# The layer norms' gain and bias as columns of the turned rows, the residual rows finished on GpSimd

## The chip, the core and the metric

The kernel runs on one core of a Trainium2 chip. The metric is the device time of one execution in microseconds (us). Engines are named as the profile names them: PE is the TensorE matmul, PEld its weight load, DVE is VectorE, ACT is ScalarE, POOL is GpSimd, SP is SyncE, whose queue issues the large weight loads.

## The reference

The program is a first block of four sublayers (hybrid attention, dense, state space, experts; only the extra row block below touches them) and then a second block of two equal layers. One layer of the second block is:

```
def layer_norm(x, g, b):
    xf = x.astype(jnp.float32)
    mu = xf.mean(-1, keepdims=True)
    var = jnp.square(xf - mu).mean(-1, keepdims=True)
    return ((xf - mu) * lax.rsqrt(var + LN_EPS) * g + b).astype(x.dtype)

def hybrid_layer(x, w_in, ..., w_out, ln1_g, ln1_b, w_up, ffn_conv_w, ffn_conv_b, w_down, ln2_g, ln2_b, pos):
    proj = x @ w_in
    ...
    mix = jnp.concatenate([o_a, o_b], -1) @ w_out
    x = layer_norm(DEEPNORM_ALPHA * x + mix, ln1_g, ln1_b)
    hid = causal_dwconv(x @ w_up, ffn_conv_w) + ffn_conv_b
    gate, val = jnp.split(hid, 2, -1)
    ffn = (jax.nn.silu(gate) * val) @ w_down
    return layer_norm(DEEPNORM_ALPHA * x + ffn, ln2_g, ln2_b)
```

x is 256 rows by 1024, all in float32. So there are four layer norms, two in each layer. The results of three of them are multiplied by a weight matrix next (w_up, then w_in of the second layer, then w_up again); the last one is the output.

## The kernel before

The residual X lies in SBUF as `X[128, 2, 1024]`: two halves h of 128 rows each. A product with a weight needs X turned (columns on the partitions), and each float32 operand is cut into a high part (ACT copies it rounded: `HTf`, `HTm`, `uh_...`) and a low part (the rest, by a subtraction: `HTlf`, `HTlm`, `ul_...`). Each product is then three matmuls. Weights arrive in `slots`, are split unit by unit by `Units.split_hi` (ACT) and `Units.split_lo` (DVE, or POOL for the units in `on_gpsimd`), and the order of work on each engine is written out by hand: `layer(c, l)` holds one function for each engine (`tensor`, `vector`, `scalar`, `gpsimd`, `sync`), and semaphore events named by tuples join them. Each engine runs its list strictly in order.

A norm goes like this. `project_quarters` leaves four sums in PSUM, a quarter (half h, columns i) each, and the last two weight units are done quarter by quarter, so that the quarters end one after the other. `post_vector` (DVE) takes for one half two quarters (`xn<-X,ps`, `st<-xn`), the mean and variance (`mv<-st`), and then four SCALAR_TENSOR_TENSOR of 128x512 with the rows `lnr` (gain and bias, sent to all 128 partitions by POOL's DMAs): `xn<-xn,mv,lnr` and `X<-xn,rs_,lnr`, twice. `rs_` comes from ACT (`post_scalar`, two small activations behind a table load). Then the same for the other half. PE turns X with 16 transposes (L136, `k_ident,X`), ACT writes the high part from PSUM (`HTf<-ps`), DVE the low part (`HTlf<-ps,HTf`, one input in PSUM and one in SBUF), and PE waits for the last low part before the first matmul of the next product.

After norm 1 comes the up projection (`uh_ffn`); its first three units are split ahead of the norm on ACT, two of their low parts on POOL in one row (`FU.on_gpsimd = (0, 1)`). After norm 2 of layer 0 comes layer 1's input projection (`uh_in`, `HTm`), called the start of layer 1 below. After norm 2 of layer 1 one DMA writes both halves to `out`.

The first block's norms already use another form, that the change takes over: `modulated_vector`, `modulated_scalar`, `modulated_low`. There the turned rows are scaled and shifted as they leave PSUM, with one number for each partition: DVE does four 128x128 pieces of a half, ACT four, ACT copies the high part in four pieces of 128x256 (events HT 0 to 7 for both halves), and DVE makes the low part in four more, `HTl<-xn,HT`, where both inputs lie in SBUF. The helpers' lines are L132 matmul, L136 transpose, L139 activation, L145 tensor_tensor, L150 tensor_scalar, L153 scalar_tensor_tensor, L177 DMA.

## Time and profile before

| | us |
|---|---|
| median of 3 runs (lowest, highest) | 2639.32 (2631.01, 2642.67) |
| span of the profiled execution | 2637.7 |
| PE busy in it | 2425.0 (92%) |
| DVE busy | 1984.6 (75%) |
| ACT busy | 1431.5 (54%) |
| POOL busy | 210.9 (8%) |

No time of its own is given for the profiled execution besides its span; the median lies 1.6 us above the span. The two layers of the second block fill the last quarter of the span. Busy shares are averages over stages with different limits: what a change at one place is worth is read from the break in PE's work there and from what ended last before PE went on.

### The profile page before, as it was taken

Reading aid. Unit: us, or ns where it says so; the run is one execution under the profiler, and the core shown is the slowest. Engines: PE = TensorE matmul, PEld = TensorE weight load, DVE = VectorE, ACT = ScalarE, POOL = GpSimd, SP = SyncE. Lnnn points to the kernel's source line nnn. Section 1 sums busy time; section 2 is a strip of 40 time slices with the busy share of each in tenths; the row PEclk is TensorE's granted clock in tenths of the full one; section 3 lists DMA queues with packets and bytes.
Section 4 is the critical chain, followed back from the end, with each engine's and each line's share of the span. In section 5 each row is a group of like instructions: output and inputs, shape, how many; then the busy total and the mean of one; then the engine's idle time right before and its main releaser. Section 6 shows DMA issues by size and latency. Waiting matters only on the chain.

```text
span 2637.7 us, 32879 instructions
## 1 busy us (share of the span) xinstructions
PE 2425.0 (92%) x13850; PEld 2105.0 (80%) x13850; DVE 1984.6 (75%) x2208; ACT 1431.5 (54%) x1594; POOL 210.9 (8%) x265
## 2 busy tenths in 40 slices
PE   4877899898899999999999999998997999897998
PEld 3756799687777888888888888887886997886997
DVE  6756777686657888989888889886666775767675
ACT  3312443464546777767676767675444653444562
POOL 1101001000000000000000000000311110221110
PEclk8986899897889999999999999999998999998999
DMA  9652678432246999999999999995224453323551
GB/s 317 214 201 88 213 273 297 161 133 92 96 171 231 348 361 347 360 349 359 352 354 345 360 342 365 340 368 186 96 76 151 162 211 136 115 78 118 197 185 76
DMA packets 263559, 608.44 MB, mean 231 GB/s; under 512 B 18472, under 2 KB 33083, under 8 KB 263403
## 3 DMA queue, kind: packets, MB, share of 16 engines
q1 hardware_dynamic: 247808, 554.39, 58.4%
q0 software_dynamic: 14640, 51.49, 5.7%
q8 instruction: 111, 1.82, 0.3%
q10 hardware_dynamic: 954, 0.37, 0.1%
q14 instruction: 46, 0.37, 0.0%
HBM read 605.17 MB, written 1.05 MB: 230 GB/s over the span
## 4 chain that ended last, share of the span: by engine, by line
PE 80%; DVE 10%; ACT 5%; DMA 2%; issue 1%; POOL 1%; SPq 0%; PEldq 0%; PEld 0%; DVEq 0%; ACTq 0%; POOLq 0%
PE ps L132 78%; PE ps L136 2%; DVE eb L153 1%; DMA slots<-in_hyb_mod_w 1%; DVE X L153 1%; ACT L142 1%; DVE ul_in L145 1%; DVE xn L153 1%; DVE macc L153 1%; ACT uh_ffn L139 0%; DMA beside<-in_dense_mod_w 0%; ACT eb L139 0%; ACT xn L139 0%; DVE ul_ssm_w L145 0%; DVE gate L153 0%
## 5 line engine op out<-in xcount | busy, mean ns | idle before, releaser
L145 DVE TENSOR_TENSOR ul_moe_w<-slots,uh_moe_w 128x2048 fp32r<-128x2048 f32 x334 | 762.6, 2290 | 108.4 <-ACT uh_moe_w L139 108.2
L139 ACT ACTIVATE uh_moe_w<-slots 128x2048 fp32r<-128x2048 f32 x334 | 640.1, 1918 | 215.7 <-PE ps L132 188.9
L132 PE MATMUL ps<-uh_moe_w,XGh 128*128 128x512 f32 x896 | 356.6, 398 | 3.1 <-DVE XGl L145 2.1
L132 PE MATMUL ps<-uh_moe_w,XGl 128*128 128x512 f32 x896 | 349.5, 390 | 0.0
L132 PE MATMUL ps<-ul_moe_w,XGh 128*128 128x512 f32 x896 | 348.9, 389 | 0.0
L145 DVE TENSOR_TENSOR ul_ffn<-slots,uh_ffn 128x2048 fp32r<-128x2048 f32 x62 | 142.1, 2292 | 100.7 <-ACT uh_ffn L139 100.7
L132 PE MATMUL ps<-HTf,uh_ffn 128*128 128x256 f32 x704 | 201.2, 286 | 2.8 <-DVE HTlf L145 2.8
L132 PE MATMUL ps<-HTf,ul_ffn 128*128 128x256 f32 x704 | 200.8, 285 | 0.0
L132 PE MATMUL ps<-HTlf,uh_ffn 128*128 128x256 f32 x704 | 200.8, 285 | 0.0
L132 PEld LDWEIGHTS ps<-uh_moe_w,XGh 128*128 128x128 f32 x896 | 168.3, 188 | 38.8 <-DVE XGl L145 2.3
L132 PEld LDWEIGHTS ps<-uh_moe_w,XGl 128*128 128x128 f32 x896 | 168.2, 188 | 35.8
L132 PEld LDWEIGHTS ps<-ul_moe_w,XGh 128*128 128x128 f32 x896 | 168.4, 188 | 35.1 <-issue 1.7
L139 ACT ACTIVATE uh_ffn<-slots 128x2048 fp32r<-128x2048 f32 x66 | 125.7, 1911 | 96.1 <-PE ps L132 96.1
L132 PE MATMUL ps<-uh_moe_w,ehTh 128*128 128x512 f32 x448 | 177.2, 395 | 0.0
L132 PE MATMUL ps<-ul_moe_w,ehTh 128*128 128x512 f32 x448 | 174.6, 390 | 0.0
L132 PEld LDWEIGHTS ps<-HTf,uh_ffn 128*128 128x128 f32 x704 | 137.0, 195 | 3.6 <-DVE HTlf L145 3.6
L132 PE MATMUL ps<-uh_moe_w,ehTl 128*128 128x512 f32 x448 | 138.1, 389 | 0.0
L132 PEld LDWEIGHTS ps<-HTlf,uh_ffn 128*128 128x128 f32 x704 | 136.9, 194 | 0.0
L132 PEld LDWEIGHTS ps<-HTf,ul_ffn 128*128 128x128 f32 x704 | 136.8, 194 | 0.0
L145 DVE TENSOR_TENSOR ul_dense_w<-slots,uh_dense_w 128x2048 fp32r<-128x2048 f32 x33 | 75.5, 2291 | 45.0 <-ACT uh_dense_w L139 45.0
L145 DVE TENSOR_TENSOR ul_ssm_w<-slots,uh_ssm_w 128x1024 fp32r<-128x1024 f32 (+1 forms) x57 | 68.5, 1204 | 54.0 <-ACT uh_ssm_w L139 53.9
L132 PE MATMUL ps<-HTm,uh_in 128*128 128x256 f32 (+1 forms) x336 | 102.5, 305 | 7.2 <-DVE HTlm L145 4.1
(511 smaller groups left out, 5565.0 us busy)
## 6 DMA issues: line engine op xcount, KB each, us to landing
slots<-in_moe_w_gu SPq DMA_DIRECT2D x111, 2048.0 KB, 8.6
slots<-in_moe_w_down SPq DMA_DIRECT2D x56, 2048.0 KB, 8.1
slots<-in_w_up SPq DMA_DIRECT2D x20, 2048.0 KB, 7.9
...
```

The costliest lines, as they stand in the source:

```text
L132: return self.e.matmul(o, lhsT, rhs, start=start, stop=stop, skip_group_check=skip) if self.e else DONE
L136: return self.e.transpose(o, i, ident[0:n, 0:n]) if self.e else DONE
L139: return self.e.activation(o, i, f, **kw) if self.e else DONE
L142: return self.e.preload_act_table_set("natural_log_exp_and_others") if self.e else DONE
L145: return self.e.tensor_tensor(o, a, b, op) if self.e else DONE
L153: return self.e.scalar_tensor_tensor(o, a, s, b, op0, op1) if self.e else DONE
```

## The change

- Gain and bias of the norms are loaded as 64 rows of 128 in a new block `ln`, by eight more DMAs on ACT's queue at the start, and turned into columns (`v_ln`) by one more PE transpose and one more DVE copy inside the hybrid stage.
- DVE normalizes a half with one TENSOR_SCALAR of 128x1024 (`X<-xn,mv,rs_`, event z) without gain and bias. PE turns that; gain and bias are applied to the turned rows by the `modulated_...` functions on DVE and ACT, for the three norms that a product follows. The third quarter's sum is taken ahead of the first half's normalizing, and DVE's part of the modulation of half 0 ahead of the second half's.
- The residual rows themselves (needed for the next norm's sum) get gain and bias in place later, by `rows_gpsimd`: for each half a multiplication and an addition of 128x1024 on POOL, X and `lnr` in SBUF. They wait for the fourth group of transposes ("turned", 3). The next norm's DVE work waits for them, in layer 1 also the scores that overwrite `lnr`. At the end POOL does half 0 and DVE half 1, and `out` is written by two DMAs.
- One of the two early low parts on POOL goes to DVE, behind the norm; the first high part (ACT) moves to before the second group of `mixTh`, so that POOL's low part can start earlier, and the third moves behind the norm.

```diff
@@ -563,11 +563,17 @@
+def columns_ready(c, name):
+    if name in ("dense", "ssm", "moe"):
+        return c.side.v.at(("mod", name, "cols"))
+    return c.first.v.at(("mod", name, "cols") if name == "hyb" else ("cols", "ln"))
 def modulated_vector(c, e, S, name, hT, hTl, h):
...
     s1, s2 = c.s12[name]
-    side = c.first if name == "hyb" else c.side
-    e.wait_ge(*side.v.at(("mod", name, "cols")))
+    e.wait_ge(*columns_ready(c, name))
     e.wait_ge(*S.t.at(("turned", 2 * h)))
...
@@ -782,13 +788,16 @@
             at += s.shape[0]
-    now, later = ("c", "a", "m"), ("b", "g0", "f0", "h0", "g1", "f1", "h1")
+    now, later = ("c", "a", "m"), ("b", "g0", "f0", "h0", "g1", "f1", "h1", "ln")
     sc, sc_e = c.sb("sc", [128, KC]), c.sb("sc_e", [128, KC])
...
         s12[n] = [c.put(12 + i / 16 + j / 32, f"s{j + 1}_{n}", [128, KC]) for j in range(2)]
+    for l in range(2):
+        for i in (1, 2):
+            s12[f"ln{i}{l}"] = [vec[f"ln{i}_{n}{l}"] for n in ("g", "b")]
     macc = c.put(12.5, "macc", [128, D])
...
@@ -1749,7 +1758,7 @@
                 tile_tensor(e, n - AHEAD)
-            if 4 <= n < 11:
+            if 4 <= n < 12:
                 c.vectors_tensor(e, n - 4, bs)
...
@@ -2909,7 +2918,7 @@
     FU = Units(S, "ffn", up_units + down_units(("ffn", l), 22), 2048, buffers=(FUh, FUl))
-    FU.on_gpsimd = (0, 1)
+    FU.on_gpsimd = (0,)
     EARLY, OUT_EARLY, FFN_EARLY, LEAD = 2, 3, 3, 2
...
@@ -3013,6 +3023,11 @@
         e.dma_start(gnr[:, :], io["gdn_norm_g_2"][l].partition_broadcast(128)).then_inc(*tables_landed.up("tables"))
+        if l:
+            e.wait_ge(*t.at(("turned", 3)))
+            e.wait_ge(*before.rows2_landed.at("rows"))
+            for h in range(2):
+                rows_gpsimd(e, g, "X2", h)
         for n in range(LAST):
...
@@ -3021,7 +3036,11 @@
             FU.split_lo(e, n)
-        e.wait_ge(*v.at(("X", 1)))
+        e.wait_ge(*F.t.at(("turned", 3)))
+        e.wait_ge(*rows_landed.at("rows"))
+        for h in range(2):
+            rows_gpsimd(e, g, "X", h)
+        e.wait_ge(*g.now())
         for i, n in enumerate(("ln2_g_2", "ln2_b_2")):
...
@@ -3031,6 +3050,16 @@
             c.layer1.early_gpsimd(e)
+        else:
+            e.wait_ge(*v.at(("X2", "z", 0)))
+            e.wait_ge(*rows2_landed.at("rows"))
+            rows_gpsimd(e, g, "end", 0)
+    def rows_gpsimd(e, g, which, h):
+        e.tensor_tensor(X[:, h, :], X[:, h, :], lnr[:, 0, :], ALU.mult).then_inc(*g.up())
+        e.wait_ge(*g.now())
+        e.tensor_tensor(X[:, h, :], X[:, h, :], lnr[:, 1, :], ALU.add).then_inc(*g.up((which, "rows", h)))
...
@@ -3461,6 +3490,8 @@
             e.wait_ge(*t.at(("s", hf, gi, j0)))
+            if l:
+                e.wait_ge(*g.at(("X2", "rows", 1)))
             if hf:
...
@@ -3541,26 +3572,38 @@
-    def post_vector(e, which, units, landed, h):
-        for i in range(2):
-            cs = slice(i * 512, (i + 1) * 512)
-            ps = c.psum.of(key(units.name, "sum", h, i))
-            e.wait_ge(*t.at((units.name, "sum", h, i)))
-            e.scalar_tensor_tensor(xn[:, h, cs], X[:, h, cs], ALPHA, ps.t[:, :], ALU.mult, ALU.add).then_inc(*v.up())
-            c.psum.leave(key(units.name, "sum", h, i), v)
-            e.wait_ge(*v.now())
-            e.bn_stats(st[:, h, i, :], xn[:, h, cs]).then_inc(*v.up())
+    def quarter_vector(e, units, h, i):
+        cs = slice(i * 512, (i + 1) * 512)
+        ps = c.psum.of(key(units.name, "sum", h, i))
+        e.wait_ge(*t.at((units.name, "sum", h, i)))
+        e.scalar_tensor_tensor(xn[:, h, cs], X[:, h, cs], ALPHA, ps.t[:, :], ALU.mult, ALU.add).then_inc(*v.up())
+        c.psum.leave(key(units.name, "sum", h, i), v)
+        e.wait_ge(*v.now())
+        e.bn_stats(st[:, h, i, :], xn[:, h, cs]).then_inc(*v.up())
+    def mean_vector(e, which, h):
         e.wait_ge(*v.now())
         e.bn_aggr(mv[:, h, :], st[:, h, :, :].rearrange("p a b -> p (a b)")).then_inc(*v.up((which, "mv", h)))
+    def centred_vector(e, which, h):
         e.wait_ge(*v.now())
-        e.wait_ge(*landed.at("rows"))
-        for i in range(2):
-            cs = slice(i * 512, (i + 1) * 512)
-            e.scalar_tensor_tensor(xn[:, h, cs], xn[:, h, cs], mv[:, h, 0:1], lnr[:, 0, cs], ALU.subtract, ALU.mult).then_inc(*v.up())
-            e.wait_ge(*v.now())
-            e.wait_ge(*a.at((which, "rst", h)))
-            e.scalar_tensor_tensor(X[:, h, cs], xn[:, h, cs], rs_[:, h:h + 1], lnr[:, 1, cs], ALU.mult, ALU.add).then_inc(*v.up((which, h, i)))
-        v.mark((which, h))
+        e.wait_ge(*a.at((which, "rst", h)))
+        e.tensor_scalar(X[:, h, :], xn[:, h, :], mv[:, h, 0:1], ALU.subtract, rs_[:, h:h + 1], ALU.mult).then_inc(*v.up((which, "z", h)))
+    def post_vector(e, which, units, rows, first=None):
+        if rows:
+            e.wait_ge(*rows)
+        for h, i in ((0, 0), (0, 1)):
+            quarter_vector(e, units, h, i)
+        mean_vector(e, which, 0)
+        quarter_vector(e, units, 1, 0)
+        centred_vector(e, which, 0)
+        quarter_vector(e, units, 1, 1)
+        mean_vector(e, which, 1)
+        if first:
+            first(e)
+        centred_vector(e, which, 1)
...
@@ -3577,26 +3620,19 @@
     def in_ready(h, i):
-        return before.v.at(("X", h) if l == 0 else ("X2", h, i))
+        return before.v.at(("X", h) if l == 0 else ("X2", "z", h))
...
         turn_tensor(c, e, S, X, [in_ready(h, i) for h in range(2) for i in range(2)])
-        e.wait_ge(*v.at(("HT", 3)))
+        e.wait_ge(*v.at(("HT", 7 if l else 3)))
         for n in range(LAST):
...
                        lambda e: mix_tensor(e, range(4)), lambda e, n: mix_tensor(e, range(4, 8) if n == 2 else ()))
-        for n in range(4):
-            h, k0 = n // 2, n % 2 * 4
-            ps = c.banks.take(key("turned2", n))
-            e.wait_ge(*ps.was)
-            e.wait_ge(*v.at(("X", h, n % 2)))
-            for k in range(4):
-                m = e.transpose(ps.t[:, k * 128:(k + 1) * 128], X[:, h, (k0 + k) * 128:(k0 + k + 1) * 128], K["ident"])
-            m.then_inc(*t.up(("turned2", n)))
-        e.wait_ge(*v.at(("HT2", 3)))
+        turn_tensor(c, e, F, X, [v.at(("X", "z", h)) for h in range(2)])
+        e.wait_ge(*F.v.at(("HT", 7)))
         for n in range(NF):
...
@@ -3654,19 +3694,19 @@
         O.split_hi(e, 4)
+        ffn_place_free(e, 0)
+        FU.split_hi(e, 0)
         mix_scalar(e, range(4, 8))
...
             O.split_hi(e, n)
-        for n in range(FFN_EARLY):
-            ffn_place_free(e, n)
-            FU.split_hi(e, n)
+        ffn_place_free(e, 1)
+        FU.split_hi(e, 1)
         e.wait_ge(*c.layer0.g.at("ln_eps"))
         post_scalar(e, "X")
-        for n in range(4):
-            h, k0 = n // 2, n % 2 * 4
-            ps = c.psum.of(key("turned2", n))
-            e.wait_ge(*t.at(("turned2", n)))
-            e.activation(hF[:, k0:k0 + 4, h * 128:(h + 1) * 128], ps.t[:, :].rearrange("p (a t) -> p a t", t=128), AF.Copy).then_inc(*a.up(("HT2", n)))
+        for h in range(2):
+            modulated_scalar(c, e, F, f"ln1{l}", hF, h)
+        ffn_place_free(e, 2)
+        FU.split_hi(e, 2)
         for n in range(FFN_EARLY, len(FU) + AHEAD):
...
@@ -3696,7 +3736,10 @@
             early_vector(e)
-        turned_vector(c, e, S, hT, hTl)
+        if l == 0:
+            turned_vector(c, e, S, hT, hTl)
+        else:
+            low_vector(e, S, "ln20", hT, hTl)
         for n in range(LAST):
...
@@ -3709,18 +3752,11 @@
             O.split_lo(e, n)
-        for h in range(2):
-            post_vector(e, "X", O, rows_landed, h)
-        for n in range(4):
-            h, k0 = n // 2, n % 2 * 4
-            hs = slice(h * 128, (h + 1) * 128)
-            ps = c.psum.of(key("turned2", n))
-            e.wait_ge(*a.at(("HT2", n)))
-            e.tensor_tensor(hFl[:, k0:k0 + 4, hs], ps.t[:, :].rearrange("p (a t) -> p a t", t=128), hF[:, k0:k0 + 4, hs].bitcast(F32), ALU.subtract).then_inc(*v.up(("HT2", n)))
-            c.psum.leave(key("turned2", n), v)
+        post_vector(e, "X", O, g.at(("X2", "rows", 1)) if l else None, lambda e: modulated_vector(c, e, F, f"ln1{l}", hF, hFl, 0))
+        low_vector(e, F, f"ln1{l}", hF, hFl)
         for n in FU.on_gpsimd:
             e.wait_ge(*g.at(("ffn", "lo", n)))
-        for n in range(2, FFN_EARLY):
+        for n in range(1, FFN_EARLY):
             FU.split_lo(e, n)
...
@@ -3745,9 +3781,22 @@
             c.layer1.early_vector(e)
-        for h in range(2):
-            post_vector(e, "X2", FU, rows2_landed, h)
+            post_vector(e, "X2", FU, g.at(("X", "rows", 1)), lambda e: modulated_vector(c, e, c.layer1, "ln20", c.layer1.hT, c.layer1.hTl, 0))
+        else:
+            post_vector(e, "X2", FU, g.at(("X", "rows", 1)))
+            e.wait_ge(*v.now())
+            e.wait_ge(*rows2_landed.at("rows"))
+            e.tensor_tensor(X[:, 1, :], X[:, 1, :], lnr[:, 0, :], ALU.mult).then_inc(*v.up())
+            e.wait_ge(*v.now())
+            e.tensor_tensor(X[:, 1, :], X[:, 1, :], lnr[:, 1, :], ALU.add).then_inc(*v.up(("end", "rows", 1)))
+    def low_vector(e, S, name, hT, hTl):
+        modulated_low(c, e, S, hT, hTl, 0)
+        modulated_vector(c, e, S, name, hT, hTl, 1)
+        modulated_low(c, e, S, hT, hTl, 1)
+    S.hT, S.hTl = hT, hTl
     S.x_event, S.ffn, S.early_vector, S.early_scalar, S.early_gpsimd = "X2", FU, early_vector, early_scalar, early_gpsimd
...
@@ -3762,9 +3811,9 @@
             s.sync(e)
-        for h in range(2):
-            e.wait_ge(*last.v.at((last.x_event, h)))
-        e.dma_start(out[0].rearrange("(h p) d -> p h d", p=128), c.X[:, :, :]).then_inc(*x_out.up("out"))
+        for h, done in ((0, last.g), (1, last.v)):
+            e.wait_ge(*done.at(("end", "rows", h)))
+            e.dma_start(out[0][h * 128:(h + 1) * 128, :], c.X[:, h, :]).then_inc(*x_out.up("out"))
         e.wait_ge(*x_out.at("out"))
```

Three places in the order of the engines follow. In them `HTf` and `HTlf` are the high and low parts of the turned rows, `ul_ffn` a low part of w_up, `v_ln` the new columns, `lnr` the gain and bias rows, and `ps` a PSUM bank. First DVE at norm 1 of layer 0, from the mean of half 0 to the first split of w_up. Before:

```order
L171 BN_AGGR mv<-st 128x2
L153 SCALAR_TENSOR_TENSOR xn<-xn,mv,lnr 128x512
L153 SCALAR_TENSOR_TENSOR X<-xn,rs_,lnr 128x512
L153 SCALAR_TENSOR_TENSOR xn<-xn,mv,lnr 128x512
L153 SCALAR_TENSOR_TENSOR X<-xn,rs_,lnr 128x512
L145 TENSOR_TENSOR HTlf<-ps,HTf 128x4x128 x4
L145 TENSOR_TENSOR ul_ffn<-slots,uh_ffn 128x2048 x2
```

This is the second half's part (the first half's, the same without the last two rows, stands before it). In the changed kernel:

```order
L171 BN_AGGR mv<-st 128x2
L150 TENSOR_SCALAR xn<-ps,v_ln 128x128 x4
L150 TENSOR_SCALAR X<-xn,mv,rs_ 128x1024
L145 TENSOR_TENSOR HTlf<-xn,HTf 128x2x128 x4
L150 TENSOR_SCALAR xn<-ps,v_ln 128x128 x4
L145 TENSOR_TENSOR HTlf<-xn,HTf 128x2x128 x4
L145 TENSOR_TENSOR ul_ffn<-slots,uh_ffn 128x2048 x3
```

The low parts now come in eight pieces, from SBUF, four of them behind the modulation of half 1, and three splits of w_up follow where there were two. Second, POOL between the loads of `lnr` around the same norm; before:

```order
L177 DMA lnr<-in_ln_b 128x1024
L145 TENSOR_TENSOR ul_ffn<-slots,uh_ffn 128x2048 x2
L177 DMA lnr<-in_ln_g 128x1024
L177 DMA lnr<-in_ln_b 128x1024
L145 TENSOR_TENSOR cg_0<-cg_0,cu_0 128x256 x22
```

In the changed kernel:

```order
L177 DMA lnr<-in_ln_b 128x1024
L145 TENSOR_TENSOR ul_ffn<-slots,uh_ffn 128x2048
L145 TENSOR_TENSOR X<-X,lnr 128x1024 x4
L177 DMA lnr<-in_ln_g 128x1024
L177 DMA lnr<-in_ln_b 128x1024
L145 TENSOR_TENSOR cg_0<-cg_0,cu_0 128x256 x22
```

One split left POOL and four operations on X came, ahead of the next loads of `lnr`. Third, POOL at the start of layer 1, from layer 0's last rows to the first rotation of the queries; in the changed kernel:

```order
L174 MEMSET gb 64x256
L177 DMA hcol<-in_gdn_dt_bias 4x1
L177 DMA hcol<-in_gdn_a_log 4x1
L177 DMA reset<-const_reset 128x256
L177 DMA perm<-const_perm 128x128
L177 DMA sin<-const_sin 128x256
L177 DMA cos<-const_cos 128x256
L177 DMA levels<-const_levels 128x896
L177 DMA cmask<-const_cmask 128x128
L177 DMA gnr<-in_gdn_norm_g 128x128
L145 TENSOR_TENSOR X<-X,lnr 128x1024 x4
L145 TENSOR_TENSOR qr<-qr,cos 128x256
```

Before, the row with `X<-X,lnr` is not there and the rest is the same.

## Rows read from the trace of the kernel before

**Rows 1.** The page: the chain that ended last, shares of the span by engine.

```profile
PE 80%; DVE 10%; ACT 5%; DMA 2%; issue 1%; POOL 1%; SPq 0%; PEldq 0%; PEld 0%; DVEq 0%; ACTq 0%; POOLq 0%
```

**Rows 2.** Timeline, PE, norm 1 of layer 0: start, duration, what, [idle before, releaser].

```profile
2014.55 0.39 PE L132 MATMUL ps<-uh_out,mixTl 128*128 128x512 f32 x1
...
2029.80 0.58 PE L132 MATMUL ps<-HTf,uh_ffn 128*128 128x256 f32 x1 [1.41 <-DVE HTlf L145]
```

**Rows 3.** Timeline, POOL and then DVE, same place.

```profile
2009.77 9.55 POOL L145 TENSOR_TENSOR ul_ffn<-slots,uh_ffn 128x2048 fp32r<-128x2048 f32 x2 [21.01 <-ACT uh_ffn L139]
...
2012.97 0.70 DVE L168 BATCH_NORM_STATS2 st<-xn 128x6 f32<-128x512 f32 x1
...
2013.95 1.01 DVE L153 SCALAR_TENSOR_TENSOR xn<-xn,mv,lnr 128x512 f32<-128x512 f32 x1
2015.24 4.62 DVE L153 SCALAR_TENSOR_TENSOR X<-xn,rs_,lnr 128x512 f32<-128x512 f32 x1 [0.28 <-ACT rs_ L139]
```

**Rows 4.** Timeline, DVE and POOL, near the end of layer 0's up projection.

```profile
2162.74 2.29 DVE L145 TENSOR_TENSOR ul_ffn<-slots,uh_ffn 128x2048 fp32r<-128x2048 f32 x1 [0.62 <-ACT uh_ffn L139]
2164.95 0.96 DVE L145 TENSOR_TENSOR fhTl<-cg,fhTh 128x256 fp32r<-128x256 f32 x1
2166.12 0.42 DVE L145 TENSOR_TENSOR fhTl<-cg,fhTh 128x256 fp32r<-128x256 f32 x1 [0.20 <-ACT fhTh L139]
...
2160.99 0.75 POOL L145 TENSOR_TENSOR cg<-cg,cu 128x256 f32<-128x256 f32 x1 [3.27 <-ACT cg L139]
2163.40 2.24 POOL L145 TENSOR_TENSOR cg<-cg,cu 128x256 f32<-128x256 f32 x1 [1.67 <-ACT cg L139]
```

**Rows 5.** Timeline, the dense stage's norm, half 1: DVE, then PE.

```profile
298.26 0.75 DVE L150 TENSOR_SCALAR xn<-X,rst 128x1024 f32<-128x1024 f32 x1 [0.50 <-ACT rst L139]
300.29 1.37 DVE L150 TENSOR_SCALAR xn<-ps,s_dense 128x128 f32<-128x128 f32 x4 [1.27 <-PE ps L136]
301.57 2.76 DVE L145 TENSOR_TENSOR HTl<-xn,HT 128x256 fp32r<-128x256 f32 x8
...
299.16 1.94 PE L136 MATMUL ps<-k_ident,xn 128*128 128x128 f32 x8 [2.85 <-DVE xn L150]
304.39 0.58 PE L132 MATMUL ps<-HT,uh_dense_w 128*128 128x256 f32 x1 [3.29 <-DVE HTl L145]
```

**Rows 6.** Timeline, start of layer 1: PE, then POOL.

```profile
2218.28 1.04 PE L136 MATMUL ps<-k_ident,X 128*128 128x128 f32 x8
...
2226.28 0.43 PE L132 MATMUL ps<-HTm,uh_in 128*36 128x256 f32 x1 [1.41 <-DVE HTlm L145]
...
2223.40 0.54 POOL L177 DMA_DIRECT2D gnr<-in_gdn_norm_g  x1
```

**Rows 7.** Timeline, POOL in layer 0's mixer: two of 128x512.

```profile
1865.56 2.49 POOL L145 TENSOR_TENSOR Ci<-AAb,levels 128x512 f32<-128x512 f32 x2
```

**Rows 8.** Timeline, end of the program: PE, DVE, SP's queue; the output's landing.

```profile
2627.67 0.39 PE L132 MATMUL ps<-uh_ffn,fhTl 128*128 128x512 f32 x1
...
2632.49 0.75 DVE L153 SCALAR_TENSOR_TENSOR X<-xn,rs_,lnr 128x512 f32<-128x512 f32 x1
2633.33 0.39 SPq L177 DMA_DIRECT2D out<-X  x1
...
DMA to landing us min/median/max: 4.0/4.0/4.0
```

**Rows 9.** Timeline, the output projection before norm 1: DVE, then PE.

```profile
2002.87 1.23 DVE L145 TENSOR_TENSOR ul_out<-slots,uh_out 128x1024 fp32r<-128x1024 f32 x1 [0.35 <-ACT uh_out L139]
...
2006.84 0.39 PE L132 MATMUL ps<-ul_out,mixTh 128*128 128x512 f32 x1
```

**Rows 10.** Timeline, ACT at the start, and PE in the hybrid stage.

```profile
11.09 1.28 ACT L142 ACT_TABLE_LOAD   x1 [7.65 <-issue]
18.80 1.06 ACT L139 ACTIVATE xn<-X 128x1024 f32<-128x1024 f32 x1 [6.42 <-DMA X<-in_x]
...
62.08 0.24 PE L136 MATMUL ps<-k_ident,gate 88*128 88x88 f32 x1
```

More of the change, by code:

```diff
@@ L589, in modulated_scalar @@
     s1, s2 = c.s12[name]
-    side = c.first if name == "hyb" else c.side
-    e.wait_ge(*side.v.at(("mod", name, "cols")))
+    e.wait_ge(*columns_ready(c, name))
     def high(j):
@@ L775, in first @@
                           (f"fconvb{l}", r128(io["ffn_conv_b_2"][l]))]
+    parts["ln"] = [(f"ln{i}_{n}{l}", r128(io[f"ln{i}_{n}_2"][l])) for l in range(2) for i in (1, 2) for n in ("g", "b")]
     vec = c.vec = {}
@@ L1798, in vector @@
                 U.split_lo(e, n)
-            if 4 <= n < 11:
+            if 4 <= n < 12:
                 c.vectors_vector(e, n - 4)
@@ L2850, in layer @@
     before = c.again if l == 0 else c.layer0
-    S = Stage(c, f"layer{l}")
+    S, F = Stage(c, f"layer{l}"), Stage(c, f"layer{l}_ffn")
     if l == 0:
@@ L2984, in layer @@
     columns_landed, tables_landed, rows_landed, rows2_landed = [c.event_signal(f"{n}{l}_landed", 16) for n in ("columns", "tables", "norm1_rows", "norm2_rows")]
+    S.rows2_landed = rows2_landed
     def key(*what):
@@ L3646, in scalar @@
             early_scalar(e)
-        turned_scalar(c, e, S, hT)
+        if l == 0:
+            turned_scalar(c, e, S, hT)
+        else:
+            for h in range(2):
+                modulated_scalar(c, e, S, "ln20", hT, h)
         for n in range(LAST):
@@ L3659, in scalar @@
             O.split_hi(e, n)
-        for n in range(FFN_EARLY):
-            ffn_place_free(e, n)
-            FU.split_hi(e, n)
+        ffn_place_free(e, 1)
+        FU.split_hi(e, 1)
         e.wait_ge(*c.layer0.g.at("ln_eps"))
         post_scalar(e, "X")
-        for n in range(4):
-            h, k0 = n // 2, n % 2 * 4
-            ps = c.psum.of(key("turned2", n))
-            e.wait_ge(*t.at(("turned2", n)))
-            e.activation(hF[:, k0:k0 + 4, h * 128:(h + 1) * 128], ps.t[:, :].rearrange("p (a t) -> p a t", t=128), AF.Copy).then_inc(*a.up(("HT2", n)))
+        for h in range(2):
+            modulated_scalar(c, e, F, f"ln1{l}", hF, h)
+        ffn_place_free(e, 2)
+        FU.split_hi(e, 2)
         for n in range(FFN_EARLY, len(FU) + AHEAD):
@@ L3698, in vector @@
             early_vector(e)
-        turned_vector(c, e, S, hT, hTl)
+        if l == 0:
+            turned_vector(c, e, S, hT, hTl)
+        else:
+            low_vector(e, S, "ln20", hT, hTl)
         for n in range(LAST):
@@ L3747, in vector @@
             c.layer1.early_vector(e)
-        for h in range(2):
-            post_vector(e, "X2", FU, rows2_landed, h)
+            post_vector(e, "X2", FU, g.at(("X", "rows", 1)), lambda e: modulated_vector(c, e, c.layer1, "ln20", c.layer1.hT, c.layer1.hTl, 0))
+        else:
+            post_vector(e, "X2", FU, g.at(("X", "rows", 1)))
[9 more added lines that the diff above has]
+    S.hT, S.hTl = hT, hTl
     S.x_event, S.ffn, S.early_vector, S.early_scalar, S.early_gpsimd = "X2", FU, early_vector, early_scalar, early_gpsimd
```

## The prediction

> **What bounds the kernel now.** PE carries 80% of the chain that ended last [rows 1] and is busy for 92% of the span; the change leaves its matmuls as they are (one small transpose is added). So I looked at the places where PE stands still around the four layer norms, and asked at each which engine ends last before PE goes on. At norm 1 of layer 0 PE ends the output projection at 2014.94 (2014.55 and 0.39) and begins w_up at 2029.80, when DVE's last low part is done: 14.9 us [rows 2]. Layer 1's norm 1 is the same within 0.1 us. At the start of layer 1 it ends at 2218.28 and begins again at 2226.28: 8.0 us [rows 6]. At the end the last residual row is done at 2633.24 and the write is issued at 2633.33 [rows 8].
>
> What the reader is to see in norm 1 is one long row: `X<-xn,rs_,lnr` of 128x512 took 4.62 us, [rows 3], where its like takes 0.75 [rows 8]. Beside it POOL ran its two splits, 2009.77 to 2019.32, and DVE's row ends just behind them. DVE's rows with one input in SBUF (`st<-xn`, 0.70) passed during the same splits without delay; the two that read both inputs from SBUF (1.01 and 4.62) did not. So a DVE instruction with two SBUF inputs waits while POOL computes on SBUF. It goes both ways, and the one that waits goes next [rows 4]: POOL's `cg<-cg,cu` came at 2163.40 into a DVE split and took 2.24 us (0.75 where nothing was in its way); and DVE's own next instruction, there at 2164.95, did not pass it: it took 0.96 instead of 0.42, until just behind POOL's end at 2165.64. The two engines took turns. In rows 3 too: DVE's 1.01 us row got in between POOL's two splits.
>
> **The change, part by part.**
>
> *Norm 1 without the meeting with POOL.* The early split leaves the norm's stretch, so the 3.9 us of waiting (4.62 less 0.75) go. After the mean of half 0 (2013.9) DVE has: a quarter 1.4 (0.69 and 0.70), normalizing half 0 0.75, the last quarter 1.4, the mean 0.25, four scaled pieces 1.37, normalizing half 1 0.75, which ends at 2019.8. The 0.75 is from a 128x1024 TENSOR_SCALAR with one arithmetic step, the 1.37 from the dense stage [rows 5]. From there to the first matmul the dense stage has exactly the new form: normalizing ends at 299.01, first matmul at 304.39, so 5.4 us; since DVE now makes half 0's low parts before it scales half 1, I take 5.6. PE would start at 2025.4, 4.4 us before 2029.80, in each of two layers.
>
> *Start of layer 1 without the meeting.* There is no wait to win. From the last sum (2218.28): quarter 1.4, mean 0.25, pieces 1.37, normalizing 0.75, then 5.6: 2227.65, which is 1.4 us later than 2226.28. The turned rows of half 0 are ready in time (eight transposes in 1.04).
>
> *The four POOL operations.* They start when PE has turned the last group, which is about 2.05 us after half 1 is normalized (the eight transposes end at 301.10 in rows 5, 2.1 behind 299.01). A POOL operation of two SBUF inputs takes 1.25 us for 128x512 [rows 7]; 128x2048 took 9.55/2 = 4.78 with some waiting [rows 3]. Between them 128x1024 is 2.3 to 2.4; I take 2.33, so 9.3 for four. At this moment DVE has the low parts of half 1 still ahead: it scales half 1's pieces first (from PSUM, not held) and is ready for the first of four low parts, both inputs in SBUF, about 1 us after POOL's first operation began. By rows 4 each of the four waits for one POOL operation, and POOL's next waits for that low part (0.3). PE waits for the last low part. That gives, from half 1 normalized: 2.1 + 4 x 2.33 + 3 x 0.25 + 0.35 = 12.5 us, instead of 5.6: 6.9 more at each of three places. With POOL's end in front: norm 1 starts PE at 2032.3, +2.5 in each layer; the start of layer 1 at 2234.6, +8.3. There POOL's nine DMA issues end at 2223.94 [rows 6], about when the last group is turned (2224.1), so they don't delay it. What stood behind these operations has time: the loads of `lnr`, and the scores that newly wait for POOL come over 30 us later. DVE's splits of w_up (three of 2.29 instead of two) are queued behind the last low part; the second unit is first wanted one unit later, and by then POOL is done: nothing.
>
> *End.* The second half's order saves little, since the last sum comes at 2628.1 [rows 8]. Quarter, mean and the wait for ACT bring normalizing to 2630.3, or, if POOL's addition on half 0 holds it, to 2632.4. Then DVE's two 128x1024 operations with two SBUF inputs (1.22 each, as the split in rows 9): the last ends at 2634.8 or 2635.6, against 2633.24. The write landed 4.0 us behind its issue; one of half the bytes lands between 2.0 and 4.0 behind it, and I take 2.7, so 1.3 sooner [rows 8]. That makes +0.3 or +1.0 (+1.6 or +2.3 if nothing is won there); I take +0.6.
> In this place the Trainium skill has a rule that no row here shows: SBUF — State Buffer, "Who interferes with whom", says that a TENSOR_SCALAR in a two-port mode also contends with GpSimd, though it has one SBUF input. By that the end would be the +1.0, by the rows alone (one input, not held) the +0.3.
>
> *The early split.* It would now run from about 2000.8 to 2005.5 on POOL (4.65), and hold DVE's `ul_out` that came at 2002.87; that ends at 2006.6 instead of 2004.1. PE reads it at 2006.84 [rows 9]: no loss, with 0.2 us to spare. Between 0 and 1 us in each layer; I take 0.
>
> *Start of the program.* Eight DMA issues of about 0.37 us on ACT's queue move its table load from 11.09 to 14.1; it ends before X lands at 18.80. One transpose (0.24) and one copy more: +0.3 [rows 10].
>
> **Sum.** 2 x 2.5 + 8.3 + 0.6 + 0.3 = 14.2 us. The profiled span of 2637.7 becomes 2651.9; the median of the runs lies 1.6 above the span, so 2653.5. A change of 0.5% (13.2 us) is about what a measurement of this kernel can tell from no change, and the forecast stands just beyond it.
>
> **The rivals.**
> (a) *The low parts pass as a group.* The point is whether DVE, once let in, keeps its turn: its instructions follow each other every 0.34 us, and POOL's next must be there within it. POOL's addition waits for its own multiplication, so it comes a little late. If DVE passes, only the first operation costs: norm 1 starts at 2025.7 (-4.1), twice, layer 1 at 2228.0 (+1.7). Sum -8.2 + 1.7 + 0.9 = -5.6: 2633.7. If low parts read beside POOL without any waiting, it is -6.5, 2632.8. For it: a shorter instruction than any that I saw in this race. Against it: rows 4, where DVE's next was there too and lost. This one ends on the other side, not slower.
> (b) *Some turns are skipped.* There are nine turns (three at each place) of about 2.2 us in my sum beyond (a). With half of them gone: +4, 2643.5. POOL's additions may miss their turn while its second multiplication, which waits for nothing, gets it.
> (c) *More is held.* If the scaled pieces from PSUM wait as well, ACT's high parts behind them start later, +1.5 to 2 at each place; with 1 us for the early split in each layer and slower normalizing (1.22 instead of 0.75 for a step with two operations): up to +24, 2663. Against it: rows 3, where `xn<-X,ps` and `st<-xn` were not held.
> (d) *The change doesn't do what it says*, and POOL's operations come after the low parts. Against: they wait for the transposes alone. This would be (a) without the first wait.
>
> **How the numbers follow.** Taking turns throughout 0.60, own range 2649 to 2659 (0.2 us more or less for each POOL operation, the end, the early split); (b) 0.17; (a) and (d) 0.15; (c) 0.08. The likeliest gives 2653.5. The range 2633 to 2661 leaves out the upper part of (c) and a part of (a). Slower by over 0.5% means beyond 2652.5: six tenths of the likeliest (0.36) and (c): 0.45 with what noise adds. Faster by over 0.5%, below 2626, needs more than (a) gives: 0.05. The rest, 0.50, lies within: (a), (b) and four tenths of the likeliest.
>
> **What would show it.** In the trace after, at each of the three places: POOL's four `X<-X,lnr` at about 2.3 to 2.6 us each, and `HTlf<-xn,HTf` of half 1 with about 2.3 us instead of 0.42, four times; PE's first matmul some 17.4 us after the last sum at norm 1 and 16.3 at the start of layer 1. Normalizing at 0.75 and the gone 4.62 us row show the gain side. If PE's break is near 10.5 and 9.5 us, (a) holds. If PE waits in the output projection for `ul_out`, the early split was priced wrong. The prediction is wrong most of all if the turns in rows 4 were chance.

## The result and the profile after

The changed kernel takes 2658.1 us, the kernel before 2639.4 (medians of 5 runs each, side by side): the measured ratio is 1.0077, with a 95% interval of 1.0056 to 1.0098 (the two medians divided give 1.0071, inside it). One of the five runs of experiment 4 took 3123.4 us at a granted clock of 0.733, in a slow state that no other run here was in, and is left out of its ratio. The profiled execution spans 2657.5 us instead of 2637.7, 19.8 more. The page's busy times, as a reader should see them first:

```profile
span 2657.5 us, 32954 instructions
...
PE 2424.0 (91%) x13851; PEld 2105.2 (79%) x13851; DVE 2002.7 (75%) x2225; ACT 1440.7 (54%) x1630; POOL 236.1 (9%) x277
...
PE 81%; DVE 10%; ACT 5%; DMA 2%; issue 1%; POOL 1%; SPq 0%; PEldq 0%; PEld 0%; DVEq 0%; ACTq 0%; POOLq 0%
```

PE's work is the same to 1 us, so the 20 us are breaks in it. The chain's shares by engine read almost as in [rows 1] and don't show where. One has to go to the places.

**Norm 1 of layer 0.** Timeline of PE (start, duration, what, [idle before, releaser]): the last sum, the two groups of transposes, and the first matmul of w_up.

```profile
2015.98 0.39 PE L132 MATMUL ps<-uh_out,mixTl 128*128 128x512 f32 x1
2017.62 1.06 PE L136 MATMUL ps<-k_ident,X 128*128 128x128 f32 x8 [1.25 <-DVE X L150]
2021.06 1.14 PE L136 MATMUL ps<-k_ident,X 128*128 128x128 f32 x8 [2.38 <-DVE X L150]
...
2032.95 0.58 PE L132 MATMUL ps<-HTf,uh_ffn 128*128 128x256 f32 x1 [10.75 <-DVE HTlf L145]
```

The break is 16.6 us (2016.37 to 2032.95) where it was 14.9 [rows 2]. The last 10.75 us of it PE waits for DVE's low parts. In the same place POOL and DVE did this, each instruction by itself (timeline, POOL first):

```profile
2022.29 2.53 POOL L145 TENSOR_TENSOR X<-X,lnr 128x1024 f32<-128x1024 f32 x1 [15.51 <-PE ps L136]
2024.89 2.40 POOL L145 TENSOR_TENSOR X<-X,lnr 128x1024 f32<-128x1024 f32 x1
2027.26 2.54 POOL L145 TENSOR_TENSOR X<-X,lnr 128x1024 f32<-128x1024 f32 x1
2029.88 2.40 POOL L145 TENSOR_TENSOR X<-X,lnr 128x1024 f32<-128x1024 f32 x1
...
2022.19 0.43 DVE L145 TENSOR_TENSOR HTlf<-xn,HTf 128x256 fp32r<-128x256 f32 x1 [0.52 <-ACT HTf L139]
2022.54 2.56 DVE L145 TENSOR_TENSOR HTlf<-xn,HTf 128x256 fp32r<-128x256 f32 x1
2025.02 1.35 DVE L150 TENSOR_SCALAR xn<-ps,v_ln 128x128 f32<-128x128 f32 x4
2026.30 1.28 DVE L145 TENSOR_TENSOR HTlf<-xn,HTf 128x256 fp32r<-128x256 f32 x1
2027.51 2.58 DVE L145 TENSOR_TENSOR HTlf<-xn,HTf 128x256 fp32r<-128x256 f32 x1
2030.01 2.56 DVE L145 TENSOR_TENSOR HTlf<-xn,HTf 128x256 fp32r<-128x256 f32 x1
2032.49 0.41 DVE L145 TENSOR_TENSOR HTlf<-xn,HTf 128x256 fp32r<-128x256 f32 x1
```

Read the two engines against each other. A low part takes 0.43 us alone and 2.56 to 2.58 where a POOL operation has just begun (1.28 where it came in the second half of one); each held one ends just after a POOL operation ends (2024.82 and 2025.10, 2027.29 and 2027.58, 2029.80 and 2030.09, 2032.28 and 2032.57: POOL's end, DVE's end), so each of DVE's low parts lets one of POOL's operations by. The four scaled pieces between them, from PSUM, pass at 1.35 us while POOL computes. The row of 4.62 us in [rows 3] is gone: its place is taken by one TENSOR_SCALAR of 0.81 us.

**Start of layer 1.** Timeline, PE, then POOL and DVE (four alike in one row):

```profile
2222.07 0.39 PE L132 MATMUL ps<-uh_ffn,fhTl 128*128 128x512 f32 x1
...
2226.17 1.44 PE L136 MATMUL ps<-k_ident,X 128*128 128x128 f32 x8 [2.83 <-DVE X L150]
...
2238.50 0.43 PE L132 MATMUL ps<-HTm,uh_in 128*36 128x256 f32 x1 [10.90 <-DVE HTlm L145]
...
2227.80 0.54 POOL L177 DMA_DIRECT2D gnr<-in_gdn_norm_g  x1
2228.36 9.81 POOL L145 TENSOR_TENSOR X<-X,lnr 128x1024 f32<-128x1024 f32 x4
...
2229.19 9.26 DVE L145 TENSOR_TENSOR HTlm<-xn,HTm 128x256 fp32r<-128x256 f32 x4
```

All four low parts of half 1 are held: 9.26 us for what takes 4 x 0.42 without POOL. The break is 16.0 us (2222.46 to 2238.50). Before, it was 7.8 from the end of the last sum (2218.44); the 8.0 of [rows 6] count from the first transpose (2218.28).

**The end.** Timeline: PE's last matmul, then POOL, DVE and SP's queue, and the landing of the two writes behind their issue.

```profile
2643.72 0.39 PE L132 MATMUL ps<-uh_ffn,fhTl 128*128 128x512 f32 x1
...
2643.77 2.35 POOL L145 TENSOR_TENSOR X<-X,lnr 128x1024 f32<-128x1024 f32 x1 [52.47 <-DVE X L150]
2646.20 2.34 POOL L145 TENSOR_TENSOR X<-X,lnr 128x1024 f32<-128x1024 f32 x1
...
2642.88 0.81 DVE L150 TENSOR_SCALAR X<-xn,mv,rs_ 128x1024 f32<-128x1024 f32 x1
...
2646.47 2.61 DVE L150 TENSOR_SCALAR X<-xn,mv,rs_ 128x1024 f32<-128x1024 f32 x1 [0.67 <-ACT rs_ L139]
2649.12 2.48 DVE L145 TENSOR_TENSOR X<-X,lnr 128x1024 f32<-128x1024 f32 x2
...
2648.56 3.43 SPq L177 DMA_DIRECT2D out<-X  x2
...
DMA to landing us min/median/max: 2.6/2.6/2.6
```

The second write is issued at 2651.6 and lands 2.6 us later, at 2654.3. Yet the span ends at 2657.5: 3.2 us in which no view shows any work. POOL's last operation ended at 2648.54, 9.0 us before the end. (The trace holds one thing more, which the views don't print: a DRAIN instruction of POOL's sequencer that ends at 2657.28, 8.7 us behind that operation. DVE's DRAIN ends 0.06 us behind DVE's last row.) From the last matmul (end 2644.11) to the end of the span it is 13.4 us, against 9.7 before (2628.06 to 2637.7, [rows 8]).

**Where the 19.8 us are**, each from PE's rows, as break after less break before, and the stretches between them likewise:

| place | before | after | difference |
|---|---|---|---|
| up to the last sum ahead of norm 1, layer 0 | 2014.9 | 2016.4 | +1.4 |
| break at norm 1, layer 0 | 14.9 | 16.6 | +1.7 |
| w_up and w_down, layer 0 | 188.6 | 189.5 | +0.9 |
| break at the start of layer 1 | 7.8 | 16.0 | +8.2 |
| layer 1 to its norm 1 | 198.3 | 201.0 | +2.7 |
| break at norm 1, layer 1 | 14.9 | 16.5 | +1.6 |
| w_up and w_down, layer 1 | 188.6 | 188.1 | -0.5 |
| last matmul to the end | 9.7 | 13.4 | +3.7 |

### The profile page after: what moved, and what is told of

Read it like the earlier page. It is cut to its first block, busy times and chain, and to the rows that moved or that the text cites. A ratio compares the mean times of both kernels' runs of the same rounds, so it can differ in the third digit from the quotient of the medians.

```text
span 2657.5 us, 32954 instructions
## 1 busy us (share of the span) xinstructions
PE 2424.0 (91%) x13851; PEld 2105.2 (79%) x13851; DVE 2002.7 (75%) x2225; ACT 1440.7 (54%) x1630; POOL 236.1 (9%) x277
## 4 chain that ended last, share of the span: by engine, by line
PE 81%; DVE 10%; ACT 5%; DMA 2%; issue 1%; POOL 1%; SPq 0%; PEldq 0%; PEld 0%; DVEq 0%; ACTq 0%; POOLq 0%
PE ps L132 79%; PE ps L136 2%; DVE eb L153 1%; DMA slots<-in_hyb_mod_w 1%; DVE HTlf L145 1%; ACT xn L139 1%; DVE ul_in L145 1%; ACT L142 1%; DMA beside<-in_dense_mod_w 1%; DVE xn L150 1%; DVE macc L153 1%; DVE HTlm L145 0%; ACT eb L139 0%; DVE ul_ssm_w L145 0%; DVE gate L153 0%
## 5 line engine op out<-in xcount | busy, mean ns | idle before, releaser
L132 PE MATMUL ps<-HTf,uh_ffn 128*128 128x256 f32 x704 | 201.8, 287 | 21.5 <-DVE HTlf L145 21.5
L132 PE MATMUL ps<-HTm,uh_in 128*128 128x256 f32 (+1 forms) x336 | 102.5, 305 | 16.5 <-DVE HTlm L145 13.4
```

The source lines that it names most:

```text
L132: return self.e.matmul(o, lhsT, rhs, start=start, stop=stop, skip_group_check=skip) if self.e else DONE
```

## The experiments

The questions were: are the turns with POOL the whole loss at the three breaks (theory), or do other parts of the new form cost (rival)? What makes the end 3.7 us longer? Is the 2.7 us in layer 1's mixer the change's? And what is the new form itself worth at norm 1? Each ratio below is to the kernel before, run alongside: its median was 2642.0 us beside experiments 1 to 4 and 2638.5 beside 5 to 8. A ratio and the quotient of two medians differ by up to 0.0008.

**1. POOL's rows behind the last low part, at all three places.** They wait for event HT 7 instead of the last transposes:

```diff
-            e.wait_ge(*t.at(("turned", 3)))
+            e.wait_ge(*v.at(("HT", 7)))
...
-        e.wait_ge(*F.t.at(("turned", 3)))
+        e.wait_ge(*F.v.at(("HT", 7)))
```

> The changed kernel, but POOL's four operations on X wait for the last low part of the turned rows instead of for the last transposes, at both norms 1 and at the start of layer 1. Theory (taking turns): the low parts of half 1 take 0.42 us each and the breaks of PE fall from 16.6, 16.2 and 16.5 us to about 10.5, 9.6 and 10.5 us, so some 19 us less than the changed kernel's 2658: about 2639, and the kernel is no longer slower than the one before. Rival (the new form itself is long: more and shorter instructions on DVE and ACT): the breaks stay above 15 us, 2655 or more. Second rival (POOL's operations only move the collision): DVE's splits of the next product are held, PE stands still one or two units later, and half of the 19 us comes back, 2648.

Measured: 2640.8 us, ratio to the kernel before 0.9990 (0.9976 to 1.0004), so no loss is left that can be told from noise: the 3.7 us at the end and 1.6 at the start of layer 1 are still in it, and the 4.4 us won at each norm 1 pay for them. The breaks are 10.5, 9.5 and 10.5 us. Its timeline at the start of layer 1, PE's first matmul and POOL:

```profile
2226.50 0.43 PE L132 MATMUL ps<-HTm,uh_in 128*36 128x256 f32 x1 [3.83 <-DVE HTlm L145]
...
2226.53 11.37 POOL L145 TENSOR_TENSOR X<-X,lnr 128x1024 f32<-128x1024 f32 x4 [3.63 <-DVE HTlm L145]
```

PE waits 3.83 us for the low parts instead of 10.90, and POOL starts behind. POOL's four now take 11.4 us, as they meet DVE's splits of weights (the first `ul_in` of 128x1024 takes 3.04 us there and 1.21 in the changed kernel). No cost to PE is to be seen: the stretch to the next norm 1 takes 200.7 us, 201.0 in the changed kernel.

**2. The same at the start of layer 1 alone** (the first of the two edits above).

> The changed kernel with POOL's four operations behind the last low part at the start of layer 1 alone; norms 1 as changed. Theory (taking turns, each place by itself): the break at the start of layer 1 falls from 16.2 to about 9.6 us, the two at norm 1 stay at 16.5: about 2651.5. Rival (the places are not independent): a gain under 4 or over 9 us.

Measured: 2649.5, ratio 1.0025 (1.0007 to 1.0043). Breaks 16.6, 9.5, 16.5: each place loses by itself and the losses add up, 6.1 and 6.1 at the norms, 6.6 at the start of layer 1 (16.0 less 9.5, the last digit by the unrounded rows).

**3. POOL's operations cut into four pieces** of 256 columns, sixteen instead of four at each place.

```diff
-        e.tensor_tensor(X[:, h, :], X[:, h, :], lnr[:, 0, :], ALU.mult).then_inc(*g.up())
+        for j in range(4):
+            cs = slice(j * 256, (j + 1) * 256)
+            e.tensor_tensor(X[:, h, cs], X[:, h, cs], lnr[:, 0, cs], ALU.mult).then_inc(*g.up())
```

(the addition likewise; each of its four pieces waits for POOL's operation before it, the multiplication's pieces wait for nothing)

> The changed kernel with each of POOL's operations of 128x1024 on X cut into four of 128x256, at the same place in its queue (16 where there were 4, about 0.73 us each by the page before, so 11.7 us in all instead of 9.3). Theory (one low part waits for one POOL instruction, whatever it is): a low part waits about 0.7 instead of 2.2 us, and the breaks fall by some 4.5 to 5 us each: about 2644. Rival (DVE is held until POOL's run is over, or gets in only by chance): POOL's longer total makes the breaks longer by 2 us each, 2664 or more.

Measured: 2646.0, ratio 1.0023 (1.0007 to 1.0039). PE at norm 1 of layer 0, and POOL's pieces there:

```profile
2023.09 0.58 PE L132 MATMUL ps<-HTf,uh_ffn 128*128 128x256 f32 x1 [4.97 <-DVE HTlf L145]
...
2018.20 18.91 POOL L145 TENSOR_TENSOR X<-X,lnr 128x256 f32<-128x256 f32 x16 [15.76 <-PE ps L136]
```

The breaks are 11.1, 11.6 and 11.5 us, where whole operations gave 16.6, 16.0 and 16.5, and none in the way gave 10.5, 9.5 and 10.5 (run 1). POOL's work behind the same event has not become less, so the price goes by the length of its single instructions and not by their sum. At the two norms no low part takes over 0.95 us: there each waits at most for the one piece that is running. At the start of layer 1 one does not. Timeline, DVE's first low part of half 1 and the pieces of POOL beside it:

```profile
2218.64 2.21 DVE L145 TENSOR_TENSOR HTlm<-xn,HTm 128x256 fp32r<-128x256 f32 x1
...
2218.49 2.08 POOL L145 TENSOR_TENSOR X<-X,lnr 128x256 f32<-128x256 f32 x3
```

The piece that runs and the two behind it all pass (2218.49 to 2220.57) before it is let in, and the next three low parts take 0.94 to 0.95 us. It came in where POOL made a pause of 0.07 us, ahead of the first addition. This is most of why this break is 2.1 us over run 1's, and those at the norms only 0.5 and 1.1. So a low part mostly pays for one POOL instruction, but one that follows without a pause may go first. What decides it isn't shown: in the changed kernel POOL's third operation followed the second without a pause (2027.26 and 2027.29 above), and DVE got in between them.

The end is longer, 16.9 us behind the last matmul. POOL's eight pieces there take 8.22 us where the two operations took 4.76, and the span again ends 9.0 us behind the last of them (2632.78 to 2641.8).

**4. The end on DVE.** DVE multiplies and adds both halves' rows at the end; POOL has nothing to do there.

```diff
-            e.wait_ge(*v.at(("X2", "z", 0)))
-            e.wait_ge(*rows2_landed.at("rows"))
-            rows_gpsimd(e, g, "end", 0)
...
-            post_vector(e, "X2", FU, g.at(("X", "rows", 1)))
+            post_vector(e, "X2", FU, g.at(("X", "rows", 1)), lambda e: end_rows(e, 0))
+            end_rows(e, 1)
```

> The changed kernel with the last half 0's two operations on DVE (ahead of the second half's normalizing), so that POOL has no work at the end. Theory (POOL's own wind-up at the end of the program takes some 8.7 us behind its last operation and is now the last to end): the span ends about 0.4 us behind the landing of the second write, as before the change. DVE's last operation comes 0.6 us later (2.4 more work, 1.8 us of held normalizing gone), the end 2.3 us earlier than in the changed kernel: about 2655.8. Rival (the two writes make the tail long): no gain, or 0.6 us lost.

Measured: 2657.3 (2656.8 without the run of 3123.4 us), ratio 1.0065 (1.0042 to 1.0088); the interval can't tell 3 us. The trace can: from the last matmul (end 2640.62) to the end of the span it is 10.7 us, where the changed kernel has 13.4. Timeline, DVE's last rows:

```profile
2644.87 0.81 DVE L150 TENSOR_SCALAR X<-xn,mv,rs_ 128x1024 f32<-128x1024 f32 x1
2645.71 2.48 DVE L145 TENSOR_TENSOR X<-X,lnr 128x1024 f32<-128x1024 f32 x2
```

The same TENSOR_SCALAR takes 0.81 us here and 2.61 beside POOL. DVE's last row ends at 2648.2, 7.6 us behind the last matmul; in the changed kernel, with half the rows on POOL, it ended 7.5 behind it. The help from POOL is worth 0.1 us, and the span ends 2.7 us later with it.

**5. Both together**, 1 and 4.

> The changed kernel with POOL's rows behind the last low part at all three places, and with DVE ending both halves at the end of the program, so that POOL has no work there. If the two causes are separate and add, the time lies 17.3 us (rows behind) and 2.8 us (POOL's wind-up at the end) below the changed kernel: breaks of 10.5, 9.5 and 10.5 us, 10.7 us from the last matmul to the end, and about 2 us less than the kernel before (ratio 0.998 to 1.000). If part of the end's cost was POOL slowing DVE and not the wind-up, the last stretch stays over 11.5 us.

Measured: 2634.8, ratio 0.9982 (0.9966 to 0.9999). Breaks 10.5, 9.5, 10.5, and 10.7 at the end, all as expected: the two causes are separate. The time is 3.7 us under the kernel before. The end is still 1.0 us longer than before (10.7 for 9.7).

**6. The new form at the two norms 1 alone**, with POOL's rows behind the last low part; norm 2 of both layers, the start of layer 1 and the end as before.

```diff
-            for h in range(2):
-                rows_gpsimd(e, g, "X2", h)
...
-        e.wait_ge(*F.t.at(("turned", 3)))
+        e.wait_ge(*F.v.at(("HT", 7)))
...
-            rows_gpsimd(e, g, "end", 0)
```

> The new form at the two norms 1 alone (with POOL's rows behind the last low part), norm 2 of both layers and the end as before. If the new form gains at norm 1 what the run with the rows behind showed (14.9 to 10.5 us of break) and only loses at the start of layer 1 and at the end, the breaks are 10.5, 7.9 and 10.5 us and the last stretch 9.7: about 8.8 us under the kernel before (ratio 0.9967). If the slower mixer of layer 1 (201 for 198.3 us) comes from the wait and the rows at its start, it goes too (198.3); if it stays, the gain is 6 us.

Measured: 2634.0, ratio 0.9981 (0.9961 to 1.0000). Breaks 10.5, 7.8, 10.5, end 9.7, as expected. The time is 4.5 us under the kernel before, where 6 were expected if layer 1's mixer stays slow. And it does: the stretch to layer 1's norm 1 stays long, 201.5 us, with nothing of the change at its start.

**7. The early split alone**, in the kernel before: one low part of w_up on POOL ahead of the norm, one on DVE behind it, ACT's order as in the change, the norms in the old form.

```diff
-    FU.on_gpsimd = (0, 1)
+    FU.on_gpsimd = (0,)
...
         O.split_hi(e, 4)
+        ffn_place_free(e, 0)
+        FU.split_hi(e, 0)
         mix_scalar(e, range(4, 8))
```

> The kernel before with the early split part alone: one low part of w_up on POOL ahead of the norm, one back on DVE behind it, ACT's third high part behind the norm; the norms in the old form. Theory: the gain of the change at norm 1 is the row of 4.62 us that met POOL's splits, and the new form itself is worth little: the breaks at norm 1 come to 11.0 us (14.9 less 3.9), the time to about 7.8 us under the kernel before (ratio 0.997). Rival: the new form (columns, one normalizing operation) makes the gain; then the breaks stay over 13 us here.

Measured: 2632.2, ratio 0.9975 (0.9960 to 0.9990), the lowest median of all, though the intervals of runs 5 and 6 overlap with this one; 6.3 us under the kernel before, 7.8 expected. PE's first matmul at norm 1 of layer 0, and DVE's row that had taken 4.62 us (timeline):

```profile
2025.84 0.58 PE L132 MATMUL ps<-HTf,uh_ffn 128*128 128x256 f32 x1 [1.41 <-DVE HTlf L145]
...
2015.15 0.75 DVE L153 SCALAR_TENSOR_TENSOR X<-xn,rs_,lnr 128x512 f32<-128x512 f32 x1
...
2001.14 4.62 POOL L145 TENSOR_TENSOR ul_ffn<-slots,uh_ffn 128x2048 fp32r<-128x2048 f32 x1 [12.55 <-ACT uh_ffn L139]
```

The breaks at both norms 1 are 10.5 us, within 0.1 of what the new form reaches in runs 1, 5 and 6. The 4.4 us are 3.9 from the row of 4.62 us (0.75 here), 0.3 from the row of 1.01 us ahead of it in [rows 3] (0.75 here), and 0.2 from `rs_`, which now comes in time. At norm 1 all of the net gain is the early split's: whatever the columns and the single normalizing operation win there, they lose again. At the start of layer 1, where no meeting was to be won, they cost 1.6 us even in the best order tried (9.5 for 7.9). The early split is itself several edits (one low part off POOL, the other earlier, ACT's order); they were not run apart.

**8. One tiny POOL operation at the very end** of the kernel before: a memset of 128x1 behind DVE's last row.

```diff
+        else:
+            e.wait_ge(*v.at(("X2", 1)))
+            e.memset(ln_eps[:, :], LN_EPS).then_inc(*g.up())
```

> The kernel before with one tiny memset (128x1) on POOL behind DVE's last row of the whole program, and nothing else. Theory: POOL's program ends some 8.7 us behind its last operation, whatever that is, and the execution ends no sooner: the stretch from the last matmul to the end grows from 9.7 to about 14.2 us (last row 5.2 behind the last matmul, memset 0.2, 8.7), +4.5 us. Rival: the longer end of the changed kernel comes from the work of the rows and the two writes; then this run shows no difference, 9.7 us.

Measured: 2646.2, ratio 1.0026 (1.0006 to 1.0045). Timeline: PE's last matmul, POOL's memset, the issue of the output.

```profile
2629.36 0.39 PE L132 MATMUL ps<-uh_ffn,fhTl 128*128 128x512 f32 x1
...
2635.00 0.10 POOL L174 MEMSET lneps<- 128x1 f32 x1 [58.05 <-DVE X L153]
...
2635.03 0.39 SPq L177 DMA_DIRECT2D out<-X  x1
```

The span is 2644.1: it ends 9.0 us behind the memset's end, while a write issued at 2635.03 had landed by 2639.0. From the last matmul to the end it is 14.3 us (14.2 expected).

The span ends 9.0 us (8.98) behind POOL's last operation with either of two very different ones, a memset of 128x1 and an addition of 128x1024, and in all five traces where POOL works last (the changed kernel and runs 1, 2, 3 and 8). Most of it is the DRAIN of POOL's sequencer: it ends at 2643.85 here. In the kernel before it also ends 8.7 us behind POOL's last operation (2575.26), and there over 50 us of the program are still to come. What it does in that time isn't shown. The median rose by 7.7 us, 4.5 expected; the interval of 1.6 to 11.9 holds both.

This run also settles most of the 2.7 us in layer 1's mixer. Its code there is that of the kernel before, and yet the stretch takes 201.1 us. Two of PE's rows (timeline) and two windows (us of PE, PEld, DVE, ACT and POOL, then the granted clock, DMA share and GB/s) show why, first of the kernel before, then of run 8:

```profile
2268.01 2.52 PE L132 MATMUL ps<-qk 128*128 128x128 f32 x16 [1.81 <-DVE qk L145]
...
2277.76 2.38 PE L132 MATMUL ps<-k_ident,Ci 128*128 128x128 f32 x16 [2.38 <-POOL Ci L145]
...
2267.00:2273.00 6.00, 4.99 (x28) 4.81 (x29) 5.31 (x8) 3.44 (x6) 2.26 (x2) 0.72 0.01 3
2277.00:2282.00 5.00, 4.17 (x32) 3.93 (x33) 3.97 (x7) 0.00 (x0) 2.67 (x3) 1.00 0.00 0
```

```profile
2266.63 2.05 PE L132 MATMUL ps<-qk 128*128 128x128 f32 x16 [1.80 <-DVE qk L145]
...
2276.40 3.79 PE L132 MATMUL ps<-k_ident,Ci 128*128 128x128 f32 x16 [3.98 <-POOL Ci L145]
...
2267.00:2273.00 6.00, 5.42 (x46) 5.08 (x44) 5.89 (x10) 3.04 (x5) 2.29 (x2) 1.00 0.01 3
2277.00:2282.00 5.00, 5.00 (x24) 4.82 (x24) 3.07 (x6) 0.00 (x0) 1.44 (x2) 0.52 0.00 0
```

In the kernel before's profiled execution the granted clock was down (0.72) at `qk` and back at 1.00 for `k_ident,Ci`; in run 8 it is the other way round, 1.00 and then 0.52, near the lower of the clock's two levels, 1.2 of 2.4 GHz. From the start of `qk` to that of `k_ident,Ci` both take 9.8 us, since PE waits for POOL there in any case: slower matmuls ahead of that wait are hidden (it is 2.38 us instead of 3.98), and slower ones behind it are not (3.79 for 2.38). Matmul by matmul, run 8 is level with the kernel before at the start of `k_ident,Ci`, 2.2 us behind it 3 us later, and loses 0.4 more at the output projection, again at a lower granted clock (0.66 for 0.83 over 10 us). In the changed kernel the clock falls elsewhere once more (0.79 in 2258 to 2266, for 1.00 in the same place before), and the 2.7 us come as 1.1 up to `k_ident,Ci`, 1.2 behind it and 0.4 at the output projection. The nine other traces lie between 199.6 and 201.8 us in this stretch; the one profiled execution of the kernel before, at 198.3, is the low one. The 2.7 us are a difference between executions, not the change's.

## Why the prediction was right

It named 2653.5 us, 14.2 over the profiled time, with the turns between POOL and DVE as the likeliest course; it came to 2658.1, inside the range. The turns are what happened, at all three places. That the sum of the places came so near (15.2 measured, see below) is partly luck: the norms were put 1.7 us too high and the end 3.1 too low. Point by point:

- **Norm 1 without the meeting**, expected to start PE 4.4 us sooner: 4.4 (14.9 to 10.5, runs 1 and 6), and by run 7 the split alone does it.
- **Start of layer 1 without the meeting**, expected +1.4: +1.6 (7.8 to 9.5).
- **The POOL operations**, 2.33 us each expected: 2.40 to 2.54, since each also lets one low part by. Turns at all places: the price expected was 6.9 at each of three places and measured 6.1, 6.6 and 6.1 (changed kernel less run 1). That the norms lost 1.7 and 1.6 us instead of 2.5 comes from POOL's start. The prediction took it 2.1 us behind half 1's normalizing, from the dense stage, where the eight transposes took 1.94 us [rows 5] at a granted clock of 0.50. Here they took 1.14 at 0.90, and POOL began 1.3 us behind (2021.01 to 2022.29). So its first operation already met the last low part of half 0, which the prediction had not seen, its fourth ended sooner, and the last low part passed freely (0.41). At the start of layer 1 the transposes ended at 2227.61, 1.5 us behind normalizing (2226.11), but POOL began at 2228.36, just behind the last of its DMA issues (2228.34). The prediction had said that these don't delay it. They did, by 0.75 us; so POOL began 2.2 us behind normalizing after all, and the loss is 8.2 where 8.3 stood. Rival (a), passing as a group, would have given the breaks of run 1; rival (b) would have shown low parts of 0.42 between POOL's operations, and the only free one is the last.
- **Scaled pieces from PSUM not held**: right, 1.35 us beside POOL. So of rival (c) nothing came, but for normalizing at 0.81 instead of 0.75.
- **The early split**, expected 0 on the path: POOL took 4.61 us, DVE's `ul_out` was held (4.71 us for two, timeline row below), and the output projection ran 26.1 and 26.2 us from its first transposes to the last sum in the two layers, where the kernel before has 25.9 twice and the untouched code of run 8 has 26.0 and 26.5. No cost beyond that spread is to be seen.

```profile
2004.29 4.71 DVE L145 TENSOR_TENSOR ul_out<-slots,uh_out 128x1024 fp32r<-128x1024 f32 x2 [0.35 <-ACT uh_out L139]
```

- **Start of the program**: ACT's table load went to 13.91 (14.1 expected), ahead of the landing of X, as expected. The first stretch differs by 1.4 us, but over all traces it lies between 2008.8 and 2018.3, so its +0.3 can't be told.
- **The end was the term that was mis-sized**: +0.6 expected, +3.7 measured. Its parts: DVE's TENSOR_SCALAR was held by POOL's addition, 2.61 us for 0.81, and the last write was issued 7.5 us behind the last matmul instead of 5.3. That was the upper bound of the prediction. The Trainium skill, SBUF — State Buffer, "Who interferes with whom", had said that a TENSOR_SCALAR in a two-port mode contends with GpSimd too, though it has one SBUF input; the trace agrees that it is held, with 2.61 against 0.81; in which mode it ran no run shows. The write landed after 2.6 us (2.7 taken). What no term held is POOL's 9.0 us behind its last operation. Before, POOL's last operation lay 62 us ahead of the end and this was hidden; the change made POOL work at the end, and so the end of the program became POOL's: 2648.54 + 9.0 = 2657.5, 3.2 us behind the landing.

With the measured sizes the places of the change come to 1.7 + 8.2 + 1.6 + 3.7 = 15.2 us. The medians differ by 18.7, with an interval of 14.8 to 25.9 that holds both; no place explains the remaining 3.5 us. The other kernels' medians lie 1.3 us below to 4.3 us above what their breaks add up to, run 8 at +7.7 for +4.6, with intervals of 4 to 6 us each way. So it may be nothing but the measurement, or something small in every execution; that was not settled.
